# Sample attention's end in a two-layer decoder step: last batch's probabilities turned one group ahead, value projection of both heads of a pair in one product

## The chip, the cores and the metric

The kernel runs on 1 core of one Trainium2 chip. The metric is the device time of one execution in microseconds (us). Of the kernel before, three runs took 2680.87, 2682.65 and 2685.53 us; the median is 2682.65.

## The reference

Two decoder layers run for a prompt of 512 tokens and for 8 sample sequences of 8 new tokens each, with shared weights. Layer 0 has multi-head latent attention, layer 1 an mLSTM; each sits between two SwiGLU feed-forward blocks and is followed by a gated input embedding. The change lies in the attention of the sample group and in what follows it. There each of the 8 sequences (a "batch") attends to 2048 cached keys in 16 pages of 128 and to its new ones:

```python
def latent_attend(q_nope, q_rope, ckv, kr, q_pos, k_pos, w_uk):
    q_abs = jnp.einsum('...qhd,rhd->...qhr', q_nope, w_uk)
    s = jnp.einsum('...qhr,...kr->...hqk', q_abs, ckv) + jnp.einsum('...qhd,...kd->...hqk', q_rope, kr)
    s = s.astype(jnp.float32) * MLA_SCALE
    s = jnp.where(k_pos[None, :] <= q_pos[:, None], s, -jnp.inf)
    p = jax.nn.softmax(s, axis=-1).astype(ckv.dtype)
    return jnp.einsum('...hqk,...kr->...qhr', p, ckv)

def mla_output(o_lat, w_uv, w_out):
    b, t = o_lat.shape[0], o_lat.shape[1]
    v = jnp.einsum('bthr,rhv->bthv', o_lat, w_uv).reshape(b, t, MLA_HEADS * MLA_V)
    return v @ w_out
```

There are 16 heads, the latent rank is 256, a head's value is 64 wide, the model 1024. Everything is fp32.

## The kernel before, in words

The kernel is written out for each engine by hand: one program each for TensorE (`pe`), VectorE (`dve`), ScalarE (`act`), GpSimd (`pool`) and the DMA-issuing SyncE (`sp`). Each runs strictly in the order in which it is written, and semaphores tie them together. All 576 tokens (512 of the prompt, 64 of the samples) stand in the free dimension, features in the 128 partitions.

A dense layer is a run of tiles (`tiles`, which calls `products`). A tile is one block of 128 outputs over 576 tokens and takes two PSUM banks, 0 and 1 or 2 and 3 by turns (`slot`). A weight panel of 8 chunks is loaded by SyncE (`raw`), ScalarE rounds it to an upper part (`whi`, L1558), GpSimd takes the difference as a lower part (`wlo`, L1520); both have two buffers. For each chunk TensorE runs three products, upper by upper, upper by lower and lower by upper (L1858, L1860, L1863), each in two spans of 320 and 256 tokens: 24 groups of two passes in a tile. For the attention's output projection (`mla_out`, 8 tiles of 8 chunks) the operands are `oTh` and `oTl`, the upper and lower part of the attention's values.

The sample attention handles batch b's scores beside batch b-1's outputs, in the loop `for b in range(NB + 1)` in `mla_pes`. The functions there:

- `turn_group`: pages of the cache are turned (banks 4 and 5) and copied to `KT`.
- `scores_s`, `rope_scores`: scores of 4 groups of 512 keys in banks 0 to 3. VectorE takes maxima, ScalarE the exponentials to `S` (L386, semaphore `sex`).
- `probs_t(b, g)`: four blocks of group g's probabilities (a fifth group holds the 64 new keys, one block) are turned into bank 6 (L796, L798). VectorE copies them to one of two buffers `PTs` (`pts_copy`, L539 and L541, semaphore `pts_taken`).
- `out_s(b, g)`: the turned probabilities times the pages, into bank 7 (L812, L815).
- `scale_output` on ScalarE (L395, semaphore `o_scaled`), then `new_and_back`: the scaled output of the batch before is turned (L756) and VectorE copies it to `QA` (L551); its memset or copy behind that (`nb_taken`) releases bank 7.

In the last round (b = 8) no scores are left; only batch 7's outputs run, each group's turn, copy and product in sequence. Then comes the value projection (L847): for each of 16 heads, two products over the latent rank, `wuv` for a pair of heads as stationary operand and one head's 64 columns of `QA` (a step of 16 values between neighbours) as moving one, 8 heads to a bank, banks 0 and 1. Of the 128 result rows each head needs 64. ScalarE writes the upper part `oTh` from PSUM (L411), VectorE the lower part `oTl` (L595, semaphore `sv_lo`), and TensorE enters `tiles("mla_out", ...)`, a loop of two rounds of four tiles, when all four pieces are there:

```python
            pe.wait_ge(sv_lo, 4)
            tiles("mla_out", 8, 1, lambda n: oTh[:, n, :], lambda n: oTl[:, n, :], 2, 4)
```

Of the kernel before, what the change touches and what calls it, by code (L numbers as in the profile page):

```python
# [79 lines left out]
def hybrid_step(nc, ins, outs):  # L80
    I = ins
    with ExitStack() as ctx:
# [236 lines left out]
        def mla_acts(act, upper, root, square, norm):  # L319
# [86 lines left out]
            for q in (0, 1):  # L406
                act.wait_ge(sv_ready, q + 1)
                for s in (0, 1):
                    rows = slice(64 * s, 64 * s + 64)
                    src = ps[rows, q, :].rearrange("p (j s t) -> p j s t", s=2, t=TS)[:, :, s, :]  # L410
                    act.activation(oTh[rows, 4 * q:4 * q + 4, TP:T], src, ACT.Copy).then_inc(sv_hi, 1)  # L411
# [3 lines left out]
        def mla_dves(dve, v, link, rms, added):  # L415
# [119 lines left out]
            def pts_copy(b, g):  # L535
                n = 5 * b + g
                dve.wait_ge(pts_ready, n + 1)
                if g < 4:
                    dve.tensor_copy(PTs[:, n % 2, :], ps[:, 6, :]).then_inc(pts_taken, 1)  # L539
                else:  # L540
                    dve.tensor_copy(PTs[0:TS, n % 2, 0:P], ps[0:TS, 6, 0:P]).then_inc(pts_taken, 1)  # L541
# [21 lines left out]
            for b in range(NB + 1):  # L563
                if b:
                    pts_copy(b - 1, 0)
                if b < NB:
                    kt_copy(4 * b + 1)
                new_and_back(b)
                for g in range(4):
                    if b < NB:  # L570
                        group_max(b, g)
                    if b and g < 3:
                        pts_copy(b - 1, g + 1)
                    if b < NB and g < 2:
                        kt_copy(4 * b + g + 2)
                if b < NB:
                    dve.wait_ge(mx_dve, 5 * b + 5)
                    dve.tensor_reduce(out=mx[:, b % 2, 5:6], in_=mx[:, b % 2, 0:5], axis=AX.X, op=ALU.max,
                                      negate=True).then_inc(snm, 1)
                if b:  # L580
                    pts_copy(b - 1, 4)
                if b < NB - 1:
                    rope_copy(b + 1)
                    kt_copy(4 * b + 4)
                if b < NB:
                    dve.wait_ge(sex, 5 * b + 5)
                    link(dve.reduce_sum(mx[:, b % 2, 6:7], mx[:, b % 2, 8:13], AX.X))
                    dve.reciprocal(mx[:, b % 2, 7:8], mx[:, b % 2, 6:7]).then_inc(s_inv, 1)
            new_and_back(NB + 1)
            for q in (0, 1):  # L590
                for s in (0, 1):
                    rows = slice(64 * s, 64 * s + 64)
                    dve.wait_ge(sv_hi, 2 * q + s + 1)
                    src = ps[rows, q, :].rearrange("p (j s t) -> p j s t", s=2, t=TS)[:, :, s, :]
                    dve.tensor_tensor(oTl[rows, 4 * q:4 * q + 4, TP:T], src,  # L595
                                      oTh[rows, 4 * q:4 * q + 4, TP:T].bitcast(F32), ALU.subtract).then_inc(sv_lo, 1)
# [3 lines left out]
        pt_banks, pv_bank = [(7, 5, 6), (4, 2, 3)], 6  # L600

# [4 lines left out]
        def mla_pes(pe, v, products, sums, tiles, xgh, xgl):  # L606
# [179 lines left out]
            def probs_t(b, g):  # L786

                n = 5 * b + g
                pe.wait_ge(sex, n + 1)
                if n:  # L790
                    pe.wait_ge(pts_taken, n)
                if g == 0 and b < NB - 1:
                    pe.wait_ge(krp_c, b + 2)
                if g < 4:
                    for k in range(4):
                        ins = tr(ps[:, 6, k * P:(k + 1) * P], S[:, b % 2, g * 512 + k * P:g * 512 + (k + 1) * P], ident)  # L796
                else:
                    ins = tr(ps[0:TS, 6, 0:P], S[:, b % 2, 2048:KEYS], ident)  # L798
                ins.then_inc(pts_ready, 1)
# [20 lines left out]
            for b in range(NB + 1):  # L820
                if b:
                    probs_t(b - 1, 0)
                if b < NB:
                    turn_group(b, 1)
                new_and_back(b)
                if b < NB:
                    rope_scores(b)
                for g in range(4):
                    if b < NB:
                        scores_s(b, g)  # L830
                    if b:
                        out_s(b - 1, g)
                        probs_t(b - 1, g + 1)
                    if b < NB and g < 2:
                        turn_group(b, g + 2)
                if b:
                    out_s(b - 1, 4)
                if b < NB - 1:
                    turn_rope(b + 1)
                    turn_group(b + 1, 0)  # L840
            new_and_back(NB + 1)
            pe.wait_ge(o_taken, NB)
            lat = QA[:, 0:2, :].rearrange("p c (t h) -> p c t h", h=NH)
            for q in (0, 1):
                for h in range(8 * q, 8 * q + 8):
                    for c in (0, 1):
                        ins = mm(ps[:, q, (h % 8) * TS:(h % 8 + 1) * TS], wuv[:, c, (h // 2) * P:(h // 2 + 1) * P],  # L847
                                 lat[:, c, :, h], start=c == 0, stop=c == 1)
                ins.then_inc(sv_ready, 1)
            pe.wait_ge(sv_lo, 4)  # L850
            tiles("mla_out", 8, 1, lambda n: oTh[:, n, :], lambda n: oTl[:, n, :], 2, 4)
# [1203 lines left out]
```

## Time and profile before

| | |
|---|---|
| median of three runs | 2682.65 us |
| the profiled execution | 2681.31 us |
| its span (first to last instruction) | 2679.6 us |
| TensorE busy | 2595.8 us, 97% of the span |
| VectorE busy | 1390.8 us, 52% |
| GpSimd busy | 920.2 us, 34% |
| ScalarE busy | 647.5 us, 24% |
| granted TensorE clock, mean | 0.984 of full speed |

A row of a profile names an engine, the line of the kernel that issued the work, the operation and the names of output and inputs. PE is TensorE's matmul, PEld its weight load, DVE VectorE, ACT ScalarE, POOL GpSimd. An fp32 product is shown as two passes, so 32 products are "x64". The chain that ended last is followed back from the last instruction: each piece is what released the next. The sample attention runs from about 671 to 877 us of the span, the value projection from 876.85, the attention's output projection from 892.1 to about 945 us.

### The profile page before, as it was taken

The page shows a single profiled execution, that of the slowest core. Times are in us where ns is not written, and L with a number is a line of the kernel's source. Part 1 is how long each engine was busy: PE and PEld are TensorE (multiplying, and loading weights), DVE is VectorE, ACT ScalarE, POOL GpSimd, SP SyncE. Part 2 cuts the span into 40 slices and gives each one's busy share as a digit, 9 for nine tenths or more (in the row PEclk, how much of TensorE's full clock was granted, in tenths as well). Part 3 has the DMA queues.
Part 4 walks back from the last instruction along what each step waited for, and adds up shares of the span by engine and source line. Part 5 has one row for each costly group of instructions (what it writes and reads, how often), then busy time and mean ns, then how long its engine had stood idle before and what let it go on. Part 6 is the DMA issues. An engine that isn't in the chain of part 4 may idle for free.

```text
span 2679.6 us, 47472 instructions
## 1 busy us (share of the span) xinstructions
PE 2595.8 (97%) x18519; PEld 2451.6 (91%) x18519; DVE 1390.8 (52%) x1590; ACT 647.5 (24%) x995; POOL 920.2 (34%) x528
## 2 busy tenths in 40 slices
PE   7999999899999999999998999999999899999998
PEld 6999999677566999999998999999997799999998
DVE  5555434777443565553347555423435575554336
ACT  3222112244222122221123222212223222221122
POOL 2334343112330234433433434343322243433342
PEclk9999999899999899999999999999999999999998
DMA  4222223212332132222232222223323222222222
GB/s 132 86 82 83 75 82 87 57 35 54 99 98 65 47 87 80 84 82 75 81 89 79 83 86 80 74 84 92 90 69 99 79 84 86 79 86 71 86 83 71
DMA packets 411258, 215.68 MB, mean 80 GB/s; under 512 B 40597, under 2 KB 408346, under 8 KB 411162
## 3 DMA queue, kind: packets, MB, share of 16 engines
q1 hardware_dynamic: 405078, 209.04, 27.1%
q10 hardware_dynamic: 2500, 3.50, 0.4%
q0 software_dynamic: 3584, 1.84, 0.4%
q8 instruction: 62, 1.02, 0.2%
q14 instruction: 34, 0.28, 0.0%
HBM read 206.57 MB, written 7.76 MB: 80 GB/s over the span
## 4 chain that ended last, share of the span: by engine, by line
PE 93%; DVE 4%; issue 1%; SPq 1%; ACT 0%; DMA 0%; ACTq 0%; DVEq 0%
PE ps L1858 26%; PE ps L1863 26%; PE ps L1860 26%; PE ps L783 2%; PE ps L812 2%; PE ps L658 1%; PE ps L736 1%; PE ps L1347 1%; PE ps L700 1%; PE ps L1359 1%; PE ps L689 1%; PE ps L847 1%; PE ps L667 0%; SPq L224 0%; PE ps L796 0%
## 5 line engine op out<-in xcount | busy, mean ns | idle before, releaser
L1520 POOL TENSOR_TENSOR wlo<-raw,whi 128x1024 fp32r<-128x1024 f32 (+3 forms) x383 | 831.3, 2171 | 1472.3 <-ACT whi L1558 1472.3
L1858 PE MATMUL ps<-xh,whi 128*128 128x320 f32 x3568 | 764.1, 295 | 10.4 <-DVE xl L1685 7.0
L1863 PE MATMUL ps<-xh,wlo 128*128 128x320 f32 x3568 | 760.5, 294 | 0.0
L1860 PE MATMUL ps<-xl,whi 128*128 128x320 f32 x3568 | 759.9, 294 | 0.0
L1558 ACT ACTIVATE whi<-raw 128x1024 fp32r<-128x1024 f32 (+3 forms) x383 | 366.3, 956 | 1497.7 <-PE ps L1863 1480.5
L1858 PEld LDWEIGHTS ps<-xh,whi 128*128 128x128 f32 x3568 | 546.1, 188 | 12.8 <-issue 4.9
L1863 PEld LDWEIGHTS ps<-xh,wlo 128*128 128x128 f32 x3568 | 545.7, 188 | 0.0
L1860 PEld LDWEIGHTS ps<-xl,whi 128*128 128x128 f32 x3568 | 545.0, 188 | 0.0
L1863 PE MATMUL ps<-uh,wlo 128*128 128x320 f32 (+1 forms) x1408 | 299.7, 294 | 0.0
L1860 PE MATMUL ps<-ul,whi 128*128 128x320 f32 (+1 forms) x1408 | 299.5, 294 | 0.0
L1858 PE MATMUL ps<-uh,whi 128*128 128x320 f32 (+1 forms) x1408 | 299.3, 293 | 0.0
L1724 DVE TENSOR_TENSOR sA<-sA,r 128x576 f32<-128x576 f32 x88 | 210.0, 2386 | 79.6 <-ACT sA L1575 79.6
L1733 DVE TENSOR_TENSOR ul<-ub,uh 128x576 f32 x88 | 224.7, 2553 | 12.5 <-DVE uh L1731 3.0
L1741 DVE SCALAR_TENSOR_TENSOR x<-ps,x 128x576 f32 x32 | 24.2, 757 | 383.7 <-PE ps L1863 383.7
L1858 PEld LDWEIGHTS ps<-uh,whi 128*128 128x128 f32 x1408 | 215.1, 188 | 0.0
L1863 PEld LDWEIGHTS ps<-uh,wlo 128*128 128x128 f32 x1408 | 215.0, 188 | 0.0
L1860 PEld LDWEIGHTS ps<-ul,whi 128*128 128x128 f32 x1408 | 214.5, 188 | 0.0
L1727 DVE TENSOR_TENSOR ub<-ps,sA 128x576 f32<-128x576 f32 x88 | 66.7, 758 | 189.1 <-PE ps L1863 188.9
L1722 DVE TENSOR_TENSOR tA<-ps,r 128x576 f32<-128x576 f32 x88 | 66.7, 757 | 164.0 <-PE ps L1863 163.1
L230 POOL DMA_DIRECT2D rp<-in_cache_krope x112 | 60.1, 536 | 101.1 <-issue 100.5
L1685 DVE SCALAR_TENSOR_TENSOR xl<-x,gn,xh (+1 forms) x56 | 82.1, 1475 | 6.1
L1692 DVE TENSOR_SCALAR xh<-x,gn x48 | 67.6, 1409 | 7.7 <-DVE x L1741 5.1
(327 smaller groups left out, 2336.5 us busy)
## 6 DMA issues: line engine op xcount, KB each, us to landing
raw<-in_w_ffa_in SPq DMA_DIRECT2D x88, 512.0 KB
raw<-in_w_ffb_in SPq DMA_DIRECT2D x88, 512.0 KB
pages<-in_cache_ckv SPq DMA_DIRECT2D x128, 128.0 KB, 2.1
raw<-in_w_ffa_out SPq DMA_DIRECT2D x32, 384.0 KB
raw<-in_w_ffb_out SPq DMA_DIRECT2D x32, 384.0 KB
raw<-in_w_mlstm_in SPq DMA_DIRECT2D x24, 512.0 KB
raw<-in_w_ffa_out SPq DMA_DIRECT2D x32, 320.0 KB
raw<-in_w_ffb_out SPq DMA_DIRECT2D x32, 320.0 KB
```

The costliest lines, as they stand in the source:

```text
L230: q.dma_start(rp[:, b % 2, n % 4, n // 4, :], I["cache_krope"][0][bass.ds(at, 1), :, :].rearrange("a k r -> (a k) r")).then_inc(rpg[b % 2] ...
L1520: pool.tensor_tensor(lo[:, 0:n, :], raw[:, p % RAW, 0:n, :], hi[:, 0:n, :].bitcast(F32), ALU.subtract).then_inc(wlo_ready, 1)
L1558: act.activation(hi[:, 0:n, :], raw[:, p % RAW, 0:n, :], ACT.Copy).then_inc(whi_ready, 1)
L1685: dve.scalar_tensor_tensor(out=lc, in0=xf, scalar=gn[:, bass.ds(c + GCOL[name], 1)], in1=hc.bitcast(F32), op0=ALU.mult, op1=ALU.subtract). ...
L1692: dve.tensor_scalar(hc, xf, gn[:, bass.ds(c + GCOL[name], 1)], None, ALU.mult).then_inc(chain, 1)
L1722: dve.tensor_tensor(tA[:, :], slot(ta), r[:, :], ALU.mult).then_inc(tile_taken, 1)
L1724: dve.tensor_tensor(sA[:, :], sA[:, :], r[:, :], ALU.mult).then_inc(chain, 1)
L1727: dve.tensor_tensor(ub[:, :], slot(ta + 1), sA[:, :], ALU.mult).then_inc(tile_taken, 1)
L1733: dve.tensor_tensor(lj, ub[:, :], hj.bitcast(F32), ALU.subtract).then_inc(u_ready, 1)
L1858: mm(out[:, t], hi[:, n, :], xh_n[:, t], start=first and n == 0, stop=False)
L1860: mm(out[:, t], hi[:, n, :], xl_n[:, t], start=False, stop=False)
L1863: ins = mm(out[:, t], lo[:, n, :], xh_n[:, t], start=False, stop=end)
```

## The change

Three things are changed. The last round is taken out of the loop and written for itself: batch 7's groups 0 and 1 are turned first, then the turn of group g+2 follows the product of group g. Odd groups of this batch go through bank 4 (`pts_bank`), and a turn waits for the copy two turns back, not one. VectorE's copies follow the same order, and batch 7's sum and reciprocal move behind the second copy and `new_and_back`. Second, the value projection takes both heads of a pair as one moving operand of 128 columns and writes banks 2 and 3. Third, tile 0 of `mla_out` waits chunk by chunk: chunks 0 to 3 for the first bank's split, chunks 4 to 7 for the second's. This form of `tiles` writes tiles 0 to 3 out and enters a loop of one round behind them.

```diff
--- before.py
+++ after.py
@@ -407,7 +407,7 @@
                 act.wait_ge(sv_ready, q + 1)
                 for s in (0, 1):
                     rows = slice(64 * s, 64 * s + 64)
-                    src = ps[rows, q, :].rearrange("p (j s t) -> p j s t", s=2, t=TS)[:, :, s, :]
+                    src = ps[rows, 2 + q, :].rearrange("p (j s t) -> p j s t", s=2, t=TS)[:, :, s, :]
                     act.activation(oTh[rows, 4 * q:4 * q + 4, TP:T], src, ACT.Copy).then_inc(sv_hi, 1)
             square("mla_out", 8)
             return norm
@@ -536,9 +536,9 @@
                 n = 5 * b + g
                 dve.wait_ge(pts_ready, n + 1)
                 if g < 4:
-                    dve.tensor_copy(PTs[:, n % 2, :], ps[:, 6, :]).then_inc(pts_taken, 1)
+                    dve.tensor_copy(PTs[:, n % 2, :], ps[:, pts_bank(b, g), :]).then_inc(pts_taken, 1)
                 else:
-                    dve.tensor_copy(PTs[0:TS, n % 2, 0:P], ps[0:TS, 6, 0:P]).then_inc(pts_taken, 1)
+                    dve.tensor_copy(PTs[0:TS, n % 2, 0:P], ps[0:TS, pts_bank(b, g), 0:P]).then_inc(pts_taken, 1)
 
             def group_max(b, g):
                 dve.wait_ge(ss_sc, 4 * b + g + 1)
@@ -560,44 +560,52 @@
                 dve.tensor_copy(QA[32 * n:32 * n + 32, 2, :], QA[0:ROPE, 2, :]).then_inc(qr_copied, 1)
             rope_copy(0)
             kt_copy(0)
-            for b in range(NB + 1):
+            for b in range(NB):
                 if b:
                     pts_copy(b - 1, 0)
-                if b < NB:
-                    kt_copy(4 * b + 1)
+                kt_copy(4 * b + 1)
                 new_and_back(b)
                 for g in range(4):
-                    if b < NB:
-                        group_max(b, g)
+                    group_max(b, g)
                     if b and g < 3:
                         pts_copy(b - 1, g + 1)
-                    if b < NB and g < 2:
+                    if g < 2:
                         kt_copy(4 * b + g + 2)
-                if b < NB:
-                    dve.wait_ge(mx_dve, 5 * b + 5)
-                    dve.tensor_reduce(out=mx[:, b % 2, 5:6], in_=mx[:, b % 2, 0:5], axis=AX.X, op=ALU.max,
-                                      negate=True).then_inc(snm, 1)
+                dve.wait_ge(mx_dve, 5 * b + 5)
+                dve.tensor_reduce(out=mx[:, b % 2, 5:6], in_=mx[:, b % 2, 0:5], axis=AX.X, op=ALU.max,
+                                  negate=True).then_inc(snm, 1)
                 if b:
                     pts_copy(b - 1, 4)
                 if b < NB - 1:
                     rope_copy(b + 1)
                     kt_copy(4 * b + 4)
-                if b < NB:
                     dve.wait_ge(sex, 5 * b + 5)
                     link(dve.reduce_sum(mx[:, b % 2, 6:7], mx[:, b % 2, 8:13], AX.X))
                     dve.reciprocal(mx[:, b % 2, 7:8], mx[:, b % 2, 6:7]).then_inc(s_inv, 1)
+            b = (NB - 1) % 2
+            pts_copy(NB - 1, 0)
+            pts_copy(NB - 1, 1)
+            new_and_back(NB)
+            dve.wait_ge(sex, 5 * NB)
+            link(dve.reduce_sum(mx[:, b, 6:7], mx[:, b, 8:13], AX.X))
+            dve.reciprocal(mx[:, b, 7:8], mx[:, b, 6:7]).then_inc(s_inv, 1)
+            for g in (2, 3, 4):
+                pts_copy(NB - 1, g)
             new_and_back(NB + 1)
             for q in (0, 1):
                 for s in (0, 1):
                     rows = slice(64 * s, 64 * s + 64)
                     dve.wait_ge(sv_hi, 2 * q + s + 1)
-                    src = ps[rows, q, :].rearrange("p (j s t) -> p j s t", s=2, t=TS)[:, :, s, :]
+                    src = ps[rows, 2 + q, :].rearrange("p (j s t) -> p j s t", s=2, t=TS)[:, :, s, :]
                     dve.tensor_tensor(oTl[rows, 4 * q:4 * q + 4, TP:T], src,
                                       oTh[rows, 4 * q:4 * q + 4, TP:T].bitcast(F32), ALU.subtract).then_inc(sv_lo, 1)
             added("mla_out", "ffb0")
 
 
         pt_banks, pv_bank = [(7, 5, 6), (4, 2, 3)], 6
+
+        def pts_bank(b, g):
+            return 4 if b == NB - 1 and g % 2 else 6
 
         def score_banks(hh):
             a, b, c = (5, 6, 7) if hh == 0 else (2, 3, 0)
@@ -786,16 +794,21 @@
             def probs_t(b, g):
 
                 n = 5 * b + g
+                bank = pts_bank(b, g)
                 pe.wait_ge(sex, n + 1)
-                if n:
+                if b == NB - 1 and g:
+                    pe.wait_ge(pts_taken, n - 1)
+                elif n:
                     pe.wait_ge(pts_taken, n)
+                if bank == 4:
+                    pe.wait_ge(kt_act, 4 * NB)
                 if g == 0 and b < NB - 1:
                     pe.wait_ge(krp_c, b + 2)
                 if g < 4:
                     for k in range(4):
-                        ins = tr(ps[:, 6, k * P:(k + 1) * P], S[:, b % 2, g * 512 + k * P:g * 512 + (k + 1) * P], ident)
+                        ins = tr(ps[:, bank, k * P:(k + 1) * P], S[:, b % 2, g * 512 + k * P:g * 512 + (k + 1) * P], ident)
                 else:
-                    ins = tr(ps[0:TS, 6, 0:P], S[:, b % 2, 2048:KEYS], ident)
+                    ins = tr(ps[0:TS, bank, 0:P], S[:, b % 2, 2048:KEYS], ident)
                 ins.then_inc(pts_ready, 1)
 
             def out_s(b, g):
@@ -817,38 +830,43 @@
 
             turn_rope(0)
             turn_group(0, 0)
-            for b in range(NB + 1):
+            for b in range(NB):
                 if b:
                     probs_t(b - 1, 0)
-                if b < NB:
-                    turn_group(b, 1)
+                turn_group(b, 1)
                 new_and_back(b)
-                if b < NB:
-                    rope_scores(b)
+                rope_scores(b)
                 for g in range(4):
-                    if b < NB:
-                        scores_s(b, g)
+                    scores_s(b, g)
                     if b:
                         out_s(b - 1, g)
                         probs_t(b - 1, g + 1)
-                    if b < NB and g < 2:
+                    if g < 2:
                         turn_group(b, g + 2)
                 if b:
                     out_s(b - 1, 4)
                 if b < NB - 1:
                     turn_rope(b + 1)
                     turn_group(b + 1, 0)
+            probs_t(NB - 1, 0)
+            probs_t(NB - 1, 1)
+            new_and_back(NB)
+            for g in range(5):
+                out_s(NB - 1, g)
+                if g < 3:
+                    probs_t(NB - 1, g + 2)
             new_and_back(NB + 1)
             pe.wait_ge(o_taken, NB)
             lat = QA[:, 0:2, :].rearrange("p c (t h) -> p c t h", h=NH)
             for q in (0, 1):
-                for h in range(8 * q, 8 * q + 8):
+                for j in range(4):
+                    m = 4 * q + j
                     for c in (0, 1):
-                        ins = mm(ps[:, q, (h % 8) * TS:(h % 8 + 1) * TS], wuv[:, c, (h // 2) * P:(h // 2 + 1) * P],
-                                 lat[:, c, :, h], start=c == 0, stop=c == 1)
+                        ins = mm(ps[:, 2 + q, j * P:(j + 1) * P], wuv[:, c, m * P:(m + 1) * P],
+                                 lat[:, c, :, 2 * m:2 * m + 2].rearrange("p t s -> p s t"), start=c == 0, stop=c == 1)
                 ins.then_inc(sv_ready, 1)
-            pe.wait_ge(sv_lo, 4)
-            tiles("mla_out", 8, 1, lambda n: oTh[:, n, :], lambda n: oTl[:, n, :], 2, 4)
+            tiles("mla_out", 8, 1, lambda n: oTh[:, n, :], lambda n: oTl[:, n, :], 2, 4,
+                  waits0=lambda n: pe.wait_ge(sv_lo, 2 if n < 4 else 4))
 
 
 
```

TensorE's order at the last batch, before (L796 and L798 turn probabilities, L812 and L815 multiply, L756 turns the scaled output back):

```order
L815 MATMUL ps<-ckt,PTs 128x256
L796 MATMUL ps<-cf,S 128x128 x4
L756 MATMUL ps<-cf,oN 128x128 x2
L812 MATMUL ps<-pages,PTs 128x256 x4
L796 MATMUL ps<-cf,S 128x128 x4
L812 MATMUL ps<-pages,PTs 128x256 x4
L796 MATMUL ps<-cf,S 128x128 x4
L812 MATMUL ps<-pages,PTs 128x256 x4
L796 MATMUL ps<-cf,S 128x128 x4
L812 MATMUL ps<-pages,PTs 128x256 x4
L798 MATMUL ps<-cf,S 64x128
L815 MATMUL ps<-ckt,PTs 128x256
```

And after the change, where the same lines are L809, L811, L825, L828 and L764:

```order
L828 MATMUL ps<-ckt,PTs 128x256
L809 MATMUL ps<-cf,S 128x128 x8
L764 MATMUL ps<-cf,oN 128x128 x2
L825 MATMUL ps<-pages,PTs 128x256 x4
L809 MATMUL ps<-cf,S 128x128 x4
L825 MATMUL ps<-pages,PTs 128x256 x4
L809 MATMUL ps<-cf,S 128x128 x4
L825 MATMUL ps<-pages,PTs 128x256 x4
L811 MATMUL ps<-cf,S 64x128
L825 MATMUL ps<-pages,PTs 128x256 x4
L828 MATMUL ps<-ckt,PTs 128x256
```

Two groups are turned ahead of the first product, and each later turn stands two products ahead of the one that needs it. The work is the same.

VectorE's order at the same place, before (L587 and L588 are batch 7's sum and reciprocal):

```order
L587 TENSOR_REDUCE mx<-mx 128x1 [waits sex]
L588 RECIPROCAL mx<-mx 128x1 [waits dve_chain]
L539 COPY PTs<-ps 128x512 [waits pts_ready]
L551 COPY QA<-ps 128x2x128 [waits new_and_back]
L557 MEMSET st 128x1
L539 COPY PTs<-ps 128x512 [waits pts_ready] x3
```

And after:

```order
L539 COPY PTs<-ps 128x512 [waits pts_ready] x2
L551 COPY QA<-ps 128x2x128 [waits new_and_back]
L557 MEMSET st 128x1
L590 TENSOR_REDUCE mx<-mx 128x1 [waits sex]
L591 RECIPROCAL mx<-mx 128x1 [waits dve_chain]
L539 COPY PTs<-ps 128x512 [waits pts_ready] x2
```

Two copies now stand ahead of the copy to `QA`, and sum and reciprocal behind it.

TensorE at the value projection and tile 0, before:

```order
L847 MATMUL ps<-QA,wuv 128x64 x32
L1899 UNCONDITIONAL_BRANCH
L1899 ISA
L1849 REGISTER_ALU
L1858 MATMUL ps<-oTh,whi 128x320
```

And after:

```order
L865 MATMUL ps<-QA,wuv 128x128 x16
L1876 MATMUL ps<-oTh,whi 128x320
L1876 MATMUL ps<-oTh,whi 128x256
L1878 MATMUL ps<-oTl,whi 128x320
L1878 MATMUL ps<-oTl,whi 128x256
```

Half as many products of twice the width, and no loop entry ahead of tile 0.

## Rows read from the trace of the kernel before

**Rows 1.** Page, the chain that ended last, by engine

```profile
PE 93%; DVE 4%; issue 1%; SPq 1%; ACT 0%; DMA 0%; ACTq 0%; DVEq 0%
```

**Rows 2.** Stretches: length, busy us (count) of PE, PEld, DVE, ACT, POOL, clock, DMA

```profile
857.00:862.50 5.50, 3.58 (x18) 2.21 (x16) 2.39 (x8) 3.47 (x11) 0.00 (x0) 1.00 0.00 0
862.50:874.60 12.10, 9.37 (x45) 7.36 (x45) 2.35 (x4) 0.00 (x0) 0.00 (x0) 1.00 0.01 1
874.60:876.80 2.20, 1.13 (x4) 0.49 (x4) 0.42 (x2) 0.47 (x1) 0.00 (x0) 1.00 0.00 0
876.80:890.40 13.60, 13.49 (x64) 13.30 (x64) 0.85 (x3) 0.77 (x3) 0.00 (x0) 0.52 0.00 0
...
892.10:901.30 9.20, 9.19 (x50) 9.20 (x51) 0.29 (x1) 0.14 (x1) 2.36 (x1) 0.69 0.21 59
```

**Rows 3.** Chain in order of time, last batch's groups: start us, us, what

```profile
862.55 1.97 PE ps L812 x8
...
864.99 0.70 DVE PTs L539
865.74 1.99 PE ps L812 x8
...
874.64 0.71 PE ps L815 x2
```

**Rows 4.** Chain in order of time, value projection to tile 0

```profile
876.85 13.51 PE ps L847 x64
...
891.68 0.43 issue
892.11 0.82 PE ps L1858 x2
892.93 0.48 PE ps L1860 x2
```

**Rows 5.** Chain in order of time, a group of a steady batch

```profile
843.62 1.73 PE ps L812 x8
845.35 0.44 PE ps L796 x4
```

**Rows 6.** Instructions in order of time, start of the last round: start us, us, engine

```profile
859.86 0.66 PE L796 MATMUL ps<-cf,S 128*128 128x128 f32 x4
...
860.97 0.48 ACT L395 ACTIVATE oN<-ps,mx 128x256 f32<-128x256 f32 x1
...
861.39 0.67 DVE L539 COPY PTs<-ps 128x512 f32<-128x512 f32 x1
...
861.98 0.42 DVE L551 COPY QA<-ps 128x256 f32<-128x256 f32 x1
```

**Rows 7.** TensorE in order of time, prompt attention (L667: value projection)

```profile
518.35 2.00 PE L667 MATMUL ps<-wuv,ckv 128*128 128x128 f32 x16
520.28 1.10 PE L676 MATMUL ps<-Q,WT 64*128 64x64 f32 x8
521.31 1.31 PE L689 MATMUL ps<-cf,PP 128*128 128x128 f32 x10
```

**Rows 8.** Instructions in order of time, ACT and POOL in the output projection

```profile
901.31 1.06 ACT L1558 ACTIVATE whi<-raw 128x1024 fp32r<-128x1024 f32 x1 [9.07 <-PE ps L1863]
907.63 1.06 ACT L1558 ACTIVATE whi<-raw 128x1024 fp32r<-128x1024 f32 x1 [5.26 <-PE ps L1863]
...
902.45 2.68 POOL L1520 TENSOR_TENSOR wlo<-raw,whi 128x1024 fp32r<-128x1024 f32 x1 [7.76 <-ACT whi L1558]
```

**Rows 9.** Busy time by stretch, earlier falls of the clock (columns as in rows 2)

```profile
662.00:665.70 3.70, 1.71 (x15) 1.27 (x14) 2.91 (x7) 1.20 (x2) 3.08 (x3) 1.00 0.06 11
665.70:669.10 3.40, 3.40 (x12) 1.54 (x11) 0.00 (x0) 0.00 (x0) 0.18 (x1) 0.50 0.00 0
...
672.50:676.00 3.50, 1.47 (x14) 1.39 (x13) 2.22 (x4) 0.93 (x2) 1.62 (x3) 1.00 0.44 119
676.00:682.70 6.70, 6.70 (x18) 2.84 (x18) 0.93 (x4) 0.27 (x1) 3.03 (x6) 0.50 0.44 134
```

## The prediction

> **What bounds the kernel now.** I read the chain that ended last first: TensorE holds 93% of the span [rows 1]. So a change pays only by what it takes out of TensorE's own order of work: passes, waits in which TensorE stands still, and time at the lower clock. The second view is the table of stretches around the change [rows 2]. From 862.5 to 874.6 us TensorE is busy 9.37 of 12.10, from 874.6 to 876.8 it is busy 1.13 of 2.20; then comes the value projection, 13.6 us, and behind a gap the first tile of the output projection (tile 0), 9.2 us. The granted clock is 1.00 (2.4 GHz) up to 876.8 and 0.52 on average over the projection: 1.2 GHz nearly throughout. The third view, the chain in order of time, shows each link of the last batch [rows 3], and the projection, the split of its result and the start of tile 0 [rows 4].
>
> **Part 1, the last batch's probabilities one group ahead.** Now each group runs strictly in turn: TensorE turns four blocks, VectorE copies them (0.70 us), TensorE multiplies. A group takes 865.74 − 862.55 = 3.2 us, and from the first product to the start of the last group's (L815) it is 874.64 − 862.55 = 12.09 us [rows 3]. Afterwards the turn of group g+2 follows the product of group g, in banks 6 and 4 by turns, and a copy has a whole product of cover. The steady batch shows what is left then: 1.73 us for a product and 0.44 us for four turns, with no gap between them [rows 5]. Last batch: 2.17 + 2.17 + (1.73 + 0.11, a single turn) + 1.73 = 7.9 us. The copy of group 2 ends some 1.4 us after its turn begins (turn with its drain 0.66 [rows 6], copy 0.70), while group 1's product of 1.73 runs: covered. Without that cover up to 0.70 us a group would come back. **Gain: 12.09 − 7.91 = 4.2 us.**
>
> Does the start move? The first product waits for the previous batch's way back: ACT's scaled output at 860.97, two turns, VectorE's copy at 861.98 [rows 6], and a memset that releases the bank. That chain is not changed, but VectorE now has two copies of probabilities ahead of this copy, where it had one. That one stood until 861.39 behind the sum of the exponentials; now it follows its turn at once (859.86 + 0.66 = 860.52 [rows 6]), and the second turn is 0.44 us behind. So the two copies run from 860.55 to about 861.95, just ahead of 861.98. I cost it at nothing; late, it costs up to 0.7 us. Sum and reciprocal of the last batch move behind this copy; they are small, and their only reader is ACT's scaling at the end, 8 us of products later. The links from L815 to the value projection stay (874.64 to 876.85, 2.2 us).
>
> **Part 2, the value projection in pairs.** Now: 64 passes of 128x64 (32 fp32 products, two passes each) in 13.51 us [rows 4], 0.211 us a pass at 1.2 GHz. After: 32 passes of 128x128. The nearest row is the prompt's value projection, L667, the same sizes and type: 16 passes from 518.35 to 520.28, 0.121 us each at the full clock [rows 7]; turns of that width take 0.44 / 4 = 0.11 [rows 5]. Behind it 8 passes with 64 contiguous columns take 520.28 to 521.31, 0.129 each [rows 7], no less. So a narrow pass seems bound by its weight load, and twice the columns fit under the same load. I take 32 × 0.121 = 3.9 us, the row of the same shape; the bounds at full clock are 32 × 0.11 = 3.5 and, were wide passes twice as long as narrow ones (half of 0.211 at 2.4 GHz, doubled), 32 × 0.211 = 6.75 us.
>
> **Part 3, the split and tile 0.** Now the split of the second half on ACT and VectorE (890.36 to 891.68) and 0.43 us of "issue", where a loop is entered, stand between projection and tile 0 [rows 4]. After, tile 0 fills banks 0 and 1 while the halves lie in 2 and 3, and its first four chunks wait only for the first half. That half is split 2.0 (16 passes with drain [rows 7]) + 1.3 = 3.3 us after the projection starts, before the projection itself ends at 3.9. The second is split at 5.3; four chunks cover up to 3.9 + 6.32 / 2 = 7.0. So the wait is gone, and nothing new is queued behind one. The next panel's upper part (ACT, 1.06 us) still comes behind the last split, its lower part on POOL takes 2.7 [rows 8]: ready near 9, against 10.2 when tile 1 begins. From projection start to tile 0: 15.26 us now [rows 4], 3.9 after. **Gain: 11.4 us.** Tiles 0 to 3 are unrolled and the loop is entered behind them, with TensorE's queue full; between nothing and the same 0.43 I take nothing. No DMA issue is added or moved within its queue.
>
> **Part 4, the clock.** Tile 0 takes 9.2 us, at a mean clock of 0.69 [rows 2]; later tiles take 907.63 − 901.31 = 6.32 [rows 8]. If the clock does not fall, **2.85 us** more. Where else did it fall? Behind 662 to 665.7 (TensorE busy 1.71 of 3.70 us) and 672.5 to 676 (1.47 of 3.50); it came back after 3.4 and 6.7 us, in which wide passes ran without a gap [rows 9]. Here the narrow passes ran without a gap for 13 us, and it stayed down. It held through 857 to 862.5 (3.58 of 5.50) and through the gapped groups [rows 2]. After the change the stretch ahead of the 2.2 us gap is dense and the projection behind it wide. I take it that the clock holds.
>
> **Sum:** 4.2 + 11.4 + 2.85 = 18.4 us, against the profiled execution's 2681.31: 2662.9. That execution lies 1.3 below the median of the runs shown (2682.65), so 2664 for a median. Later stages shift as a whole.
>
> One rule of the skill speaks against Part 2. Both forms read the moving operand (`lat`) with a step of 16 fp32 values, and no row shows such a read 128 wide. The Trainium skill, SBUF — State Buffer, the passage on cachelines in "Door 1: The DMA port swizzle", says that an access pays a penalty each time it goes to a new 16-byte line; by it every column would pay. So far the trace doesn't show that: the stepped narrow pass, 0.211 us at 1.2 GHz, is no slower in cycles than the contiguous one. Its case is rival C.
>
> **The rivals.** Mine is A.
> B, the clock falls all the same (25%): the 2.2 us gap stays. Then 3.4 to 6.7 us run at half speed [rows 9], 1.7 to 3.4 us are lost: 2666 to 2667.5. For it: two falls in this same stage behind gaps. Against: the dense stretch ahead.
> C, the stepped read costs 4 cycles a column, not 2 (10%). The present pass allows it: 64 columns in 0.211 us at 1.2 GHz is just that. At the full clock the projection takes 6.75 us, 2.9 more: 2667. With the clock down too it is 13.5 as now, only 4.2 and the 1.7 us gap are won: near 2677 (3 of the 10).
> D, Part 1 doesn't do what it says (5%): turns and copies fall back into step, since bank 4 or the second copy comes late. 4.2 us are lost: 2668.
> E, slower (3%): the clock falls in the projection and stays down in the output projection. At 1.2 GHz two passes take 0.48 us [rows 4], a tile 24 × 0.48 = 11.5, 5.2 more than 6.32. The other 15.6 us are eaten by three such tiles; with four the time is near 2688. Against it: tile 0 itself brought the clock back within 9.2 us [rows 2].
>
> **How the numbers follow.** A has 57%, with 2662.5 to 2665.5 from the bounds of the pass and the scatter of medians. The range 2661 to 2669 takes in B, C at the full clock and D; C at the low clock and E lie outside, with some misjudged sizes. 0.2% is 5.4 us, about what a measurement of this kernel can tell from no change: A, B, D and C at full clock lie beyond it. Faster 0.94, same 0.03 (C at the low clock, a part of it), slower 0.03.
>
> **What would show it.** In the profile after: groups of the last batch 2.2 us apart with no wait for the copies; the projection's 32 passes within 3.5 to 4 us; tile 0 behind them without a wait; granted clock 1.00 from 870 us on; tile 0 taking 6.3 us. A projection of 6.75 us at a clock of 1.00 would be C, at 0.50 B. I am wrong altogether if tile 0 waits for the lower part of its split or of its panel.

## The result, and the profile after

The changed kernel takes 2665.44 us (median of four runs, 2664.94 to 2666.70) against 2682.23 us of the kernel before (four runs, 2680.87 to 2685.53). The ratio is 0.9939, with a 95% interval of 0.9928 to 0.9951. The medians differ by 16.8 us; 2664 us had been forecast. The profiled execution took 2666.7 us; its span is 2664.9 us, against 2679.6.

Spans can't be subtracted for the local reading: in the run of before VectorE's last maximum (L545) starts at 857.06 us, in this one at 858.29, though nothing ahead of it was changed. I measure from that maximum to ACT's upper part (whi) of a panel of the next stage, which tile 7's last product releases, and call it the local distance. The two rows in the timeline of the kernel before (start us, us, engine):

```profile
857.06 0.69 DVE L545 TENSOR_REDUCE mx<-ps 128x1 f32<-128x512 f32 x1 [1.03 <-PE ps L783]
...
945.61 1.06 ACT L1558 ACTIVATE whi<-raw 128x1024 fp32r<-128x1024 f32 x1 [5.32 <-PE ps L1863]
```

And in that of the changed kernel:

```profile
858.29 0.69 DVE L545 TENSOR_REDUCE mx<-ps 128x1 f32<-128x512 f32 x1 [1.03 <-PE ps L791]
...
931.73 1.06 ACT L1576 ACTIVATE whi<-raw 128x1024 fp32r<-128x1024 f32 x1 [5.29 <-PE ps L1881]
```

Before it is **88.55 us**, after **73.44 us**. So 15.1 us are won between these two points. What the spans and medians differ by beyond that (a clock that fell at other places, among others) is not the change's.

The chain in order of time after the change (start us, us, what; L809 and L811 turn probabilities, L825 and L828 multiply, L865 is the value projection, L1876 and L1878 are tile 0) answers to [rows 3 to 5]:

```profile
863.78 1.97 PE ps L825 x8
865.75 0.44 PE ps L809 x4
866.18 1.73 PE ps L825 x8
867.91 0.44 PE ps L809 x4
868.35 1.73 PE ps L825 x8
870.08 0.11 PE ps L811
870.19 1.73 PE ps L825 x8
871.92 0.64 PE ps L828 x2
872.56 0.02 issue
872.58 0.48 ACT oN L395
...
873.58 0.43 DVE QA L551
874.02 0.04 issue
874.06 7.22 PE ps L865 x32
881.28 0.27 PE ps L1876 x2
881.55 0.26 PE ps L1878 x2
```

No copy of probabilities stands in the chain any more: the groups follow each other without a gap. Between the value projection and tile 0 there is neither a split nor an "issue" piece. But the projection takes 7.22 us, not 3.9. The stretches of the same execution (length, busy us of PE, PEld, DVE, ACT and POOL with counts, clock, DMA share, GB/s), which answer to [rows 2]:

```profile
862.50:870.50 8.00, 7.16 (x38) 6.10 (x39) 2.90 (x8) 0.18 (x1) 0.00 (x0) 1.00 0.01 2
870.50:872.80 2.30, 2.04 (x9) 1.20 (x7) 0.01 (x1) 0.22 (x1) 0.00 (x0) 1.00 0.00 0
...
874.00:881.30 7.30, 7.24 (x34) 7.06 (x35) 0.86 (x4) 0.76 (x2) 0.00 (x0) 0.77 0.00 0
...
884.00:890.00 6.00, 6.00 (x48) 6.00 (x47) 1.96 (x3) 1.06 (x1) 2.89 (x2) 1.00 0.31 87
```

The clock did fall, inside the projection (0.77 of full speed on average), but it was back before tile 0. In half-microsecond steps it reads 0.50 from 876.5 to 879.5, 0.86 and 0.72 in the steps on either side of that, and 1.00 beyond: 3.4 us at 1.2 GHz. The terms, from the two chains and the two timelines:

| stretch | before | after | won | forecast |
|---|---|---|---|---|
| last maximum to first product of the last batch | 5.49 | 5.49 | 0.0 | 0 |
| first product to the fifth group's | 12.09 | 8.14 | 4.0 | 4.2 |
| from there to the value projection | 2.21 | 2.14 | 0.1 | 0 |
| value projection's start to tile 0 | 15.26 | 7.22 | 8.0 | 11.4 |
| tile 0's start to the end of tile 7 | 53.50 | 50.45 | 3.05 | 2.85 |

They add up to 15.1 us. One term misses, by 3.4 us. Of the last term 0.2 us has nothing to do with the granted clock: a later tile takes 6.29 us in this execution and 6.32 in that of before, and e_contig below, with the same unrolled tiles as the changed kernel, has 6.32 again.

### The profile page after: what moved, and what is told of

Read it like the earlier page. It is cut to its first block, busy times and chain, and to the rows that moved or that the text cites. A ratio compares the mean times of both kernels' runs of the same rounds, so it can differ in the third digit from the quotient of the medians.

```text
span 2664.9 us, 47391 instructions
## 1 busy us (share of the span) xinstructions
PE 2585.9 (97%) x18487; PEld 2441.4 (92%) x18487; DVE 1390.8 (52%) x1590; ACT 647.5 (24%) x995; POOL 919.5 (35%) x528
## 4 chain that ended last, share of the span: by engine, by line
PE 93%; DVE 4%; issue 2%; SPq 1%; ACT 0%; POOL 0%; DMA 0%; DVEq 0%; POOLq 0%; ACTq 0%
PE ps L1881 26%; PE ps L1876 26%; PE ps L1878 26%; PE ps L791 2%; PE ps L825 2%; PE ps L666 1%; PE ps L744 1%; PE ps L1365 1%; PE ps L708 1%; PE ps L1377 1%; PE ps L697 1%; PE ps L675 0%; SPq L224 0%; PE ps L809 0%; PE ps L783 0%
## 5 line engine op out<-in xcount | busy, mean ns | idle before, releaser
L1876 PE MATMUL ps<-xh,whi 128*128 128x320 f32 x3568 | 762.9, 294 | 10.2 <-DVE xl L1703 6.8
L1878 PE MATMUL ps<-xl,whi 128*128 128x320 f32 x3568 | 759.5, 294 | 0.0
L1876 PEld LDWEIGHTS ps<-xh,whi 128*128 128x128 f32 x3568 | 547.3, 188 | 13.1 <-issue 4.8
L1878 PEld LDWEIGHTS ps<-xl,whi 128*128 128x128 f32 x3568 | 542.7, 188 | 0.0
L1878 PE MATMUL ps<-ul,whi 128*128 128x320 f32 (+1 forms) x1408 | 299.3, 294 | 0.0
L1876 PE MATMUL ps<-uh,whi 128*128 128x320 f32 (+1 forms) x1408 | 298.7, 293 | 0.0
L1876 PEld LDWEIGHTS ps<-uh,whi 128*128 128x128 f32 x1408 | 215.7, 188 | 0.0
L1878 PEld LDWEIGHTS ps<-ul,whi 128*128 128x128 f32 x1408 | 213.4, 188 | 0.0
```

Of the source, the lines that this page charges most:

```text
L1876: mm(out[:, t], hi[:, n, :], xh_n[:, t], start=first and n == 0, stop=False)
L1878: mm(out[:, t], hi[:, n, :], xl_n[:, t], start=False, stop=False)
```

## The experiments

Two theories for that term. **Theory S:** the wide pass is set by its moving operand, which is read with a step of 16 values, so that each value lies 64 bytes from the next. **Rival W:** it is the width or the weight load, whatever the step. A third candidate, the fallen clock, is left to e_triple. The experiments change the changed kernel, unless said otherwise.

**Neighbouring heads as column pairs** (e_pairs). Only the order of the columns changes; the split, on ScalarE and VectorE, reads them accordingly.

```diff
-                                 lat[:, c, :, 2 * m:2 * m + 2].rearrange("p t s -> p s t"), start=c == 0, stop=c == 1)
+                                 lat[:, c, :, 2 * m:2 * m + 2], start=c == 0, stop=c == 1)
...
-                    src = ps[rows, 2 + q, :].rearrange("p (j s t) -> p j s t", s=2, t=TS)[:, :, s, :]
+                    src = ps[rows, 2 + q, :].rearrange("p (j t s) -> p j s t", s=2, t=TS)[:, :, s, :]
```

> The changed kernel with the columns of the wide product in the order token, head: the two heads of a pair are neighbours in memory, so that each 16-byte line that the moving read touches gives two values, not one. Output columns come in that order too and the split reads them with a step of 2. Theory S (the wide pass of 0.226 us is set by the stepped read): passes near 0.12 us at the full clock, projection 3.9 to 4.5 us instead of 7.2, time 2662 to 2662.5 against 2665.4 of the changed kernel. If the penalty is per line and not per lone value, half of it stays: 0.17 us a pass, 5.5 us, 2663.7. Rival W (the wide pass costs this because of its width or its weight load, whatever the step): projection 7.2 us, 2665.4. A slower split would show as tile 0 waiting.

Measured: 2663.7 us (2662.45 to 2664.95), ratio to before 0.9928 (0.9912 to 0.9945). Local distance 70.06 us, 3.4 less than the changed kernel. The chain:

```profile
873.50 0.43 DVE QA L551
873.98 3.84 PE ps L865 x32
877.82 0.27 PE ps L1876 x2
878.09 0.26 PE ps L1878 x2
```

The same 32 passes over the same data take 3.84 us. Width and weights are unchanged, so rival W falls. The half penalty falls as well, but by this row alone: its forecast for the whole time, 2663.7 us, is the very median measured. The clock stayed up this time:

```profile
872.40:873.95 1.55, 0.50 (x3) 0.20 (x2) 0.43 (x2) 0.47 (x1) 0.00 (x0) 1.00 0.00 0
873.95:877.85 3.90, 3.87 (x34) 3.87 (x35) 0.84 (x2) 0.76 (x2) 0.00 (x0) 1.00 0.00 0
877.85:884.10 6.25, 6.25 (x49) 6.25 (x49) 1.38 (x3) 1.82 (x3) 2.39 (x1) 1.00 0.09 25
```

**A contiguous copy of the latents** (e_contig). VectorE's copy back writes a buffer ordered by head; `mx` and the byte that the memset writes move elsewhere to make room.

```diff
-                    src = ps[:, 7, 256:512].rearrange("p (c t) -> p c t", c=2)
-                    dve.tensor_copy(QA[:, 0:2, (b - 2) * P:(b - 1) * P], src).then_inc(o_taken, 1)
+                    src = ps[:, 7, 256:512].rearrange("p (c t h) -> p c t h", c=2, h=NH)
+                    dst = latT[:, :, :, (b - 2) * TB:(b - 1) * TB].rearrange("p c h t -> p c t h")
+                    dve.tensor_copy(dst, src).then_inc(o_taken, 1)
...
-                                 lat[:, c, :, 2 * m:2 * m + 2].rearrange("p t s -> p s t"), start=c == 0, stop=c == 1)
+                                 latT[:, c, 2 * m:2 * m + 2, :].rearrange("p s t -> p (s t)"), start=c == 0, stop=c == 1)
```

> The changed kernel with the latents copied back head by head into a buffer of their own, so that the wide product's moving operand is contiguous. VectorE's copy (0.42 us) writes with a step now. Theory S: passes 0.11 to 0.12 us at the full clock, projection 3.5 to 3.9 us, time 2662. Rival W: 7.2 us, 2665.4. If the stepped write makes the copy slower, it costs once or twice that on the path at the end, under 0.5 us.

Measured: 2663.96 us, ratio 0.9929 (0.9913 to 0.9946), local distance 70.59 us.

```profile
874.97 0.60 DVE latT L554
875.57 0.04 issue
875.61 3.84 PE ps L868 x32
```

A contiguous operand is no faster than pairs: 3.84 us both times. The stepped write makes VectorE's copy 0.60 us instead of 0.43, and that stands on the path twice, ahead of the first product and ahead of the projection (0.33 of the 0.53 us by which the local distances differ; 0.2 is the pace of the later tiles, 6.32 us each). So the column pairs, which cost nothing, are better.

**The stepped projection three times over** (e_triple), for the pass at either clock.

```diff
-            for q in (0, 1):
+            for q in (0, 1, 0, 1, 0, 1):
```

(`sv_ready` is raised in the last two rounds alone.)

> The changed kernel with its stepped wide projection done three times over (96 passes; the result is the same), to read the pass at either clock on a long stretch. Theory S in its time form: the read of one stepped value takes some 1.76 ns whatever the clock, a pass of 128 columns 0.226 us at 2.4 GHz; at 1.2 GHz two cycles a column give 0.213, so the same within 0.013 us. Rival: the read costs cycles, then 0.226 at 2.4 GHz would be 0.45 at 1.2. Projection 21.3 to 21.7 us, 2680 in all.

Measured: 2677.33 us (one run), and 21.17 us for 96 passes, both a little below what was expected. TensorE's timeline, cut off at points 2 us apart (start us, us), gives the pass at the full clock; the stretches (length, busy us of PE and PEld with counts, DVE, clock, DMA share, GB/s; the projection's instructions alone) give the clock:

```profile
873.77 0.61 PE L866 MATMUL ps<-QA,wuv 128*128 128x128 f32 x2
...
885.76 0.61 PE L866 MATMUL ps<-QA,wuv 128*128 128x128 f32 x2
```

```profile
874.00:888.00 14.00, 14.00 (x66) 13.25 (x65) 0.00 (x0) 1.00 0.00 1
870.20:873.40 3.20, 3.20 (x17) 3.20 (x16) 0.00 (x0) 0.50 0.00 0
```

A pass is shown 0.39 us long, and 66 of them touch the 14 us: (14 + 0.39) / 66 = 0.218 us from start to start. The two starts agree, 11.99 us for 55 passes, all at 2.4 GHz. The whole is 21.17 us, of which 3.42 at 1.2 GHz and 0.18 of drain; the rest, 17.57 us, is 80.6 passes, so 15.4 passes ran in the 3.42 us, 0.222 each. Read one by one, the starts of single passes in this trace lie 0.218 us apart at both clocks (means over 80 and 13 intervals, 0.219 and 0.218). The stepped pass takes **0.22 us at either clock**. The time form of theory S holds, the rival (0.45 at 1.2 GHz) doesn't, and the fallen clock isn't what made the wide pass slow.

**The old narrow product in the changed kernel** (e_narrow: part 2 undone), and the same **with contiguous operands** (e_narrow_contig: the buffer of e_contig).

```diff
-                for j in range(4):
-                    m = 4 * q + j
+                for h in range(8 * q, 8 * q + 8):
                     for c in (0, 1):
-                        ins = mm(ps[:, 2 + q, j * P:(j + 1) * P], wuv[:, c, m * P:(m + 1) * P],
-                                 lat[:, c, :, 2 * m:2 * m + 2].rearrange("p t s -> p s t"), start=c == 0, stop=c == 1)
+                        ins = mm(ps[:, 2 + q, (h % 8) * TS:(h % 8 + 1) * TS], wuv[:, c, (h // 2) * P:(h // 2 + 1) * P],
+                                 lat[:, c, :, h], start=c == 0, stop=c == 1)
```

> The changed kernel with the value projection undone: 64 passes of 64 columns again, into banks 2 and 3; turns one group ahead and the early tile 0 stay. Theory S together with a clock that falls in the projection and stays down under narrow passes: 0.211 us a pass, projection near 13 us, low clock until some us into tile 0: 6 us for the projection and up to 2.9 for tile 0 more than the changed kernel, 2671.5 to 2674.5. If the dense stretch ahead of it keeps the clock up: a pass of 64 stepped columns should take 0.113 to 0.12 us, the projection 7.2 to 7.7 us, the time 2665.5 to 2666, and then the wide product would have won nothing by itself.

> Narrow product with contiguous operands (the latents copied back head by head), turns one group ahead and early tile 0 as in the changed kernel. If the narrow pass at the lower clock is bound by its weight load (my reading) it stays at 0.205 to 0.211 us, the clock falls and stays down as with stepped operands, projection 13.2 us. Rival: the step binds it there too, then a pass falls to about 0.12 us and the projection to 7 to 8 us.

Measured: e_narrow 2675.76 us (ten runs, 2666.74 to 2680.47), a little above the first range, ratio 0.9976 (0.9965 to 0.9986), local distance 81.86; e_narrow_contig 2676.48 us (one run), local distance 81.99. The stretches of e_narrow:

```profile
871.60:873.10 1.50, 0.47 (x3) 0.20 (x2) 0.43 (x2) 0.47 (x1) 0.00 (x0) 1.00 0.00 0
873.10:886.30 13.20, 13.15 (x65) 13.15 (x66) 0.85 (x3) 0.76 (x2) 0.00 (x0) 0.54 0.01 1
886.30:892.00 5.70, 5.70 (x29) 5.70 (x29) 1.38 (x3) 1.81 (x3) 2.36 (x1) 0.58 0.02 6
```

Its first seven passes, in TensorE's timeline ahead of the fall of the clock:

```profile
873.15 1.03 PE L864 MATMUL ps<-QA,wuv 128*128 128x64 f32 x7 [0.52 <-DVE QA L551]
```

And the projection in the chain of e_narrow_contig:

```profile
872.07 13.41 PE ps L867 x64
```

The dense groups ahead don't keep the clock up: it falls under the narrow passes and stays down for 17.1 us in both, into tile 0. And the step is not what the narrow pass waits for at 1.2 GHz: contiguous it is no faster (13.41 against 13.15 us; the clock fell 0.3 us earlier in the projection there). Read one by one from the traces, the starts of narrow passes lie 0.213 us apart at 1.2 GHz and, in the few ahead of the fall, 0.112 at 2.4, stepped or contiguous (medians); at 2.4 GHz a wide pass in pairs takes 0.112 as well. So neither width nor step sets the narrow pass, but something that costs about the same cycles in every pass. The prediction took it for the weight load, which fits; no run varies the load, so that stays argued.

The merge wins 8.4 us by itself (81.86 − 73.44): 5.9 in the projection and 2.5 behind it, nearly all through the clock in tile 0. But it wins them against a narrow form at 1.2 GHz. An estimate from the passes above: at 2.4 GHz the 64 narrow ones would take 64 × 0.112 = 7.2 us, and the 32 stepped wide ones take 32 × 0.218 = 7.0. Only with pairs (3.84 us) is the merged projection shorter at the full clock too.

**Part 1 alone** (e_turns: the narrow product and, instead of the early start, the old wait).

```diff
-            tiles("mla_out", 8, 1, lambda n: oTh[:, n, :], lambda n: oTl[:, n, :], 2, 4,
-                  waits0=lambda n: pe.wait_ge(sv_lo, 2 if n < 4 else 4))
+            pe.wait_ge(sv_lo, 4)
+            tiles("mla_out", 8, 1, lambda n: oTh[:, n, :], lambda n: oTl[:, n, :], 2, 4)
```

> Part 1 alone: the turns one group ahead, with the old projection and the old wait for both halves before tile 0, which enters its loop as before. Expected by the traces: 4.0 us less than the kernel before, 2678.2. If the clock falls later or rises sooner through it, up to 3 us less again. Rival: the turns' gain is taken back elsewhere, 2682.

Measured: 2677.40 us (ten runs, 2674.64 to 2680.52), ratio 0.9979 (0.9969 to 0.9988), local distance 82.97: 5.6 us less than before. The median lies in the expected stretch, from 2678.2 us to 3 less. The groups take 8.14 us, that is the 4.0. The clock was down for 17.1 us instead of 20.5, and 1.3 more are won in tile 0, 0.3 in the projection (13.24 us).

**Part 2 alone** (e_wide) and **parts 2 and 3 without part 1** (e_proj), both made from the kernel before, with banks 2 and 3 for the split and, in e_proj, the early start. The lines below show the product alone.

```diff
-                for h in range(8 * q, 8 * q + 8):
+                for j in range(4):
+                    m = 4 * q + j
                     for c in (0, 1):
-                        ins = mm(ps[:, q, (h % 8) * TS:(h % 8 + 1) * TS], wuv[:, c, (h // 2) * P:(h // 2 + 1) * P],
-                                 lat[:, c, :, h], start=c == 0, stop=c == 1)
+                        ins = mm(ps[:, 2 + q, j * P:(j + 1) * P], wuv[:, c, m * P:(m + 1) * P],
+                                 lat[:, c, :, 2 * m:2 * m + 2].rearrange("p t s -> p s t"), start=c == 0, stop=c == 1)
```

> Part 2 alone: wide product, the old sequence of turns and the old wait before tile 0. Projection 6.8 to 7.2 us instead of 13.5, 6.3 to 6.7 us less, and tile 0 at the full clock for most of it, up to 2.9 less: 2673.5 to 2676.5 against 2682.7. If the clock falls as before and stays down through tile 0 all the same, 2676.5.

> Parts 2 and 3 without part 1: turn, copy and product of the last batch in strict sequence again, wide product and early tile 0 as in the changed kernel. The groups' stretch takes 12.1 us instead of 8.1 (4.0 more): 2669.4. If the gaps in it make the clock fall in the projection and stay down, tile 0 loses up to 2.9 more: 2672. The wide stepped pass should be 0.213 to 0.226 us at either clock, so the projection is 6.8 to 7.2 us whatever the clock.

Measured: e_wide 2676.08 us (2672.41 to 2678.86), ratio 0.998 (0.9971 to 0.999), local distance 79.70; e_proj 2671.46 us (2670.69 to 2674.98), ratio 0.9967 (0.9956 to 0.9979), local distance 77.47. The stepped projection takes 7.23 us in both, and the clock falls once, for 3.4 us, inside it:

```profile
877.40:884.70 7.30, 7.22 (x32) 6.67 (x32) 0.86 (x4) 0.76 (x2) 0.00 (x0) 0.77 0.00 0
884.70:886.50 1.80, 0.04 (x1) 0.07 (x1) 1.16 (x3) 1.74 (x3) 0.00 (x0) 1.00 0.00 0
```

That is e_wide; tile 0 starts there at the full clock even behind the gap. e_proj lies inside its range of 2669.4 to 2672, e_wide too. By local distances part 2 alone wins 8.85 us, part 3 on top 2.23 (1.8 of it the gap, the rest in the tiles) and part 1 on top of both 4.03.

**Part 3 undone** (e_late: the edit of e_turns, with the wide product kept).

> The changed kernel with part 3 undone: tile 0 waits for both halves of the split and enters its loop as before; wide product and turns one group ahead stay. By the traces 1.7 us of gap comes back (0.02 + 0.39 + 0.02 + 0.42 + 0.03 + 0.44 + 0.43), so 2667.1 against 2665.4. If the gap lets the clock fall or keeps it down, tile 0 loses up to 2.9 us more: 2670. Rival: the split was hidden anyway, 2665.4.

Measured: 2668.64 us (2666.26 to 2673.19), ratio 0.9957 (0.994 to 0.9973), local distance 78.14, 4.7 more than the changed kernel. That lies between the two forecasts, 2667.1 with the gap alone and 2670 with the clock down in tile 0. In this execution the clock fell twice:

```profile
869.50:872.90 3.40, 3.40 (x17) 3.38 (x16) 0.02 (x1) 0.41 (x2) 0.00 (x0) 0.56 0.00 0
872.90:876.00 3.10, 3.02 (x14) 2.50 (x13) 0.82 (x2) 0.40 (x2) 0.00 (x0) 0.93 0.00 0
876.00:877.70 1.70, 0.02 (x1) 0.05 (x1) 1.12 (x3) 1.65 (x3) 0.00 (x0) 0.72 0.00 0
877.70:883.60 5.90, 5.90 (x25) 5.90 (x26) 0.26 (x1) 0.12 (x1) 2.36 (x1) 0.50 0.32 87
```

1.75 us is the gap (875.93 to 877.68) and 2.9 the second fall, which is down from 876.8, inside the gap, and covers 5.9 us of tile 0. That e_wide has the same gap and no second fall leaves open when the gap does this: it was seen in one of the two kernels that have it behind the wide product, each in one execution.

**Both once more, side by side** (a_again is the changed kernel, p_again the column pairs).

> The changed kernel once more, on the same chip as the next one: 2665.4.

> The version with neighbouring heads as column pairs once more: 3.4 us below the changed kernel by the traces (projection 3.84 against 7.22), so 2662.0 to 2662.5 beside it; by the first medians only 1.7.

Measured: a_again 2670.87 us (five runs, 2667.04 to 2672.02), ratio 0.9951 (0.9938 to 0.9965), which misses the 2665.4 expected of a mere repetition; p_again 2662.78 us (2657.95 to 2663.86), ratio 0.9929 (0.9915 to 0.9942). The local distances repeat to a hundredth: 73.45 and 70.06 us. So the change and the better version do the same each time in their own place; the 5.4 us by which the changed kernel's two medians differ are made elsewhere. The profiled executions show it: in a_again VectorE's last maximum starts at 862.21 us, 3.9 later than in the first one, ahead of everything that the change touches. Part of that is the clock, 0.97 over the first 60 us, where the first one has 1.00; the rest is not traced. The two intervals still overlap by a hair. By the whole time alone the column pairs are the better version in both pairs of medians (by 1.7 and 8.1 us), and the trace gives their size: 3.4 us.

## Why the prediction was right

- **What bounds the kernel** held: everything won was won on TensorE's own order, and each term can be read off the chain.
- **Part 1** held: 12.09 became 8.14 us against 7.91 worked out. The missing 0.24 is the first product, which takes 1.97 us and not the 1.73 of a steady one, as every product of the last batch behind a wait did before (1.97 to 1.99). The start did not move (5.49 us from the last maximum in both), so the second copy cost nothing, and rival D is out; e_turns shows the 4.0 alone.
- **Part 2** is the term that was mis-sized. "32 × 0.121 = 3.9 us, the row of the same shape" took the price from L667, whose moving operand is contiguous. The projection measured 7.22 us, 0.22 us a pass. Rival C had the mechanism and the size at the full clock (6.75 us, near 2667) but told it in cycles, with 13.5 us when the clock is down; e_triple shows a time that doesn't depend on the clock. e_pairs, with 3.84 us, shows that L667's price is right once two neighbours are read one behind the other. The argument that "the stepped narrow pass […] is no slower in cycles than the contiguous one" was true and proved nothing: the narrow pass takes the same time either way (e_narrow, e_narrow_contig), because something else in it takes longer than 64 stepped reads (64 × 1.7 ns = 0.11 us, an estimate from the wide pass). 128 of them, 0.22 us, stand out.
- **Part 3** held in its mechanism: tile 0 starts right behind the last pass, with no wait and no loop entry, and the unrolled tiles cost nothing. Its figure of 11.4 us included the projection's price and came to 8.0. Its own worth is 2.2 us between e_wide and e_proj, where the clock stays up in tile 0, and 4.7 between e_late and the changed kernel, where it was down in e_late's.
- **Part 4** was right in its sum and half wrong in its reason. "I take it that the clock holds": it fell, as rival B said, for 3.4 us. But it fell inside the projection, where the stepped pass takes 0.22 us at either clock, so it cost nothing, and tile 0 ran at 2.4 GHz: 3.05 us won where 2.85 were worked out. In the three profiled executions with pair or contiguous columns the clock did not fall there at all; in all six with the stepped wide product it did. What decides that is not shown. The prediction's tally of earlier falls was also short: in the trace of before the clock fell a third time nearby, from 696.4 to 699.9 us, behind 6.4 us in which TensorE was busy for 3.7.
- The forecast of 18.4 us, less 3.3 of Part 2, is the 15.1 us measured locally. Taken from the recorded median of 2682.65 these give 2667.5 us, rival C's number and not the forecast's. The median moved by 16.8 in the first comparison and by 10.8 in a_again's, and a_again's 2670.87 lies outside the range of 2661 to 2669. So the mechanism was right but for Part 2, and that 2665.44 came within 1.5 us of the 2664 was luck: what happened outside the change's own stretch in those runs.

## What to carry to other kernels

Before an operand's price is taken from a row of the same shape, compare the step between its neighbours too: a narrow pass that waits for something else can hide a slow read that a wider one shows. When two operands are merged, choose the order in which the values that are neighbours in memory come one behind the other. Compare two forms at the clock at which each will run: at 1.2 GHz the stepped wide pass cost no more than the narrow one (0.218 against 0.213 us), at 2.4 GHz twice as much (0.218 against 0.112). And look at the work behind: here the clock stayed down under the narrow passes, and the first tile behind them lost some 2.4 us to it. Last, a change of half a per cent is judged in its own stretch of the trace: that distance repeated to 0.01 us, while two medians of the same kernel lay 5.4 us apart.

## What the runs showed of the hardware

- An fp32 pass of 128 columns takes 0.12 us at 2.4 GHz when its values come in neighbouring pairs or in one run (3.84 us for 32, e_pairs and e_contig), and 0.22 us when each value lies 64 bytes from the next, at 2.4 and at 1.2 GHz alike (e_triple). The Trainium skill, SBUF — State Buffer, cachelines in "Door 1: The DMA port swizzle", says that two hits in a 16-byte line are needed to hide the access; the trace agrees, two were enough. No other step was run, so the length of the line itself is not measured here.
- An fp32 pass of 64 columns takes 0.213 us from start to start at 1.2 GHz and 0.112 us at 2.4 GHz (the latter from the first few passes), with a step of 64 bytes (e_narrow) and contiguous (e_narrow_contig).
- With 64-column fp32 passes in the projection the clock stayed at 1.2 GHz for 17.1 us, some 4 to 5 of them in tile 0 (e_narrow, e_narrow_contig) or 2.9 behind a gap (e_turns), and for 20.5 us in the kernel before; with 128-column stepped passes it was back after 3.4 us (the changed kernel, e_wide, e_proj, e_triple). In the projection the profile shows TensorE busy without a gap under both, so its busy share doesn't tell the two apart here.
- A copy from PSUM on VectorE that writes with a step took 0.60 us instead of 0.43 (e_contig).
